# Storing the split projection weights of the prompt block through GpSimd's DMA queue

## The reference, cut to what matters

```
h = _rmsnorm(x, norm_mix_g) * (1.0 + sc1) + sh1
...
proj = jnp.einsum('btd,dc->btc', h, w_in)
```

## Time and profile before

| | |
|---|---|
| runs | 2404.28, 2408.15, 2408.19 us, median 2408.15 |
| span of the profiled execution, first to last instruction | 2406.7 us, 1.45 us under the median; its own time is not listed apart from the runs |
| TensorE / weight load / VectorE / ScalarE / GpSimd busy | 93% / 85% / 69% / 50% / 30% |
| mean granted TensorE clock | 0.969 |
| SP's DMA queue (q1, hardware) | 377.81 MB |
| GpSimd's DMA queue (q0, software) | 126.38 MB |
| prompt block's projection | about 52 to 154 us of the span |

### The profile page before, as it was taken

How to read it: one execution, slowest core, us unless ns; L and a number is a source line. 1 busy time by engine, 2 the same in 40 slices (tenths; PEclk the granted TensorE clock), 3 DMA queues, 4 the chain that set the end, 5 groups by cost and what they waited for, 6 DMA issues and landing times.

```text
span 2406.7 us, 43831 instructions
## 1 busy us (share of the span) xinstructions
PE 2242.9 (93%) x16687; PEld 2055.1 (85%) x16687; DVE 1667.3 (69%) x2936; ACT 1194.0 (50%) x1935; POOL 712.7 (30%) x654
## 2 busy tenths in 40 slices
PE   3889999999996899975999999999999999999995
PEld 3877878788785677763999999999999999999995
DVE  1879979799788766667666655665566656666585
ACT  3766364553524454431545554555445554555574
POOL 1000000000001311101354455544554455534541
PEclk8989999999998999987999999999999999999998
DMA  6987576757747566355476677666775677666986
GB/s 225 370 319 220 200 251 229 263 193 250 236 145 264 158 210 193 106 176 139 149 206 185 193 198 213 188 185 197 197 211 180 179 212 198 199 192 179 299 250 245
DMA packets 291030, 505.80 MB, mean 210 GB/s; under 512 B 27713, under 2 KB 234302, under 8 KB 275296
## 3 DMA queue, kind: packets, MB, share of 16 engines
q1 hardware_dynamic: 251792, 377.81, 48.1%
q0 software_dynamic: 39120, 126.38, 19.4%
HBM read 405.61 MB, written 98.53 MB: 209 GB/s over the span
## 4 chain that ended last, share of the span: by engine, by line
PE 60%; DVE 5%; DMA 2%; issue 1%; ACT 1%; POOL 0%; SPq 0%; DVEq 0%; POOLq 0%; ACTq 0%
PE bank L1650 19%; PE bank L1652 19%; PE bank L1651 19%; DMA out_dram<-work_exp 1%; PE bank L1904 1%; DVE work_exp L2918 1%; DVE work_proj L2558 1%; PE bank L1970 1%; PE bank L1914 1%; PE bank L1922 1%; DVE work_exp L3181 1%; PE bank L1979 0%; POOL cat_hl L1454 0%; DMA work_exp<-x_rows 0%; DVE hl_exp L3097 0%
## 5 line engine op out<-in xcount | busy, mean ns | idle before, releaser
L1650 PE MATMUL bank<-act_hl_exp,hl_exp 128*128 128x288 f32 x3072 | 909.8, 296 | 11.5 <-DVE hl_exp L3097 7.5
L1651 PE MATMUL bank<-act_hl_exp,hl_exp 128*128 128x288 f32 x3072 | 907.5, 295 | 1.0 <-issue 0.8
L1652 PE MATMUL bank<-act_hl_exp,hl_exp 128*128 128x288 f32 x3072 | 905.7, 295 | 0.0
L1650 PEld LDWEIGHTS bank<-act_hl_exp,hl_exp 128*128 128x128 f32 x3072 | 577.2, 188 | 12.5 <-DVE hl_exp L3097 9.0
L1651 PEld LDWEIGHTS bank<-act_hl_exp,hl_exp 128*128 128x128 f32 x3072 | 578.1, 188 | 2.5 <-issue 2.5
L1652 PEld LDWEIGHTS bank<-act_hl_exp,hl_exp 128*128 128x128 f32 x3072 | 579.2, 189 | 0.2 <-issue 0.2
L3097 DVE TENSOR_TENSOR hl_exp<-work_exp,hl_exp 128x1024 fp32r<-128x1024 f32 x192 | 231.3, 1226 | 205.8 <-ACT hl_exp L1238 195.4
L3097 DVE TENSOR_TENSOR hl_exp<-raw_exp,hl_exp 128x1024 fp32r<-128x1024 f32 x192 | 231.4, 1221 | 196.5 <-ACT hl_exp L1238 176.7
L2558 DVE SCALAR_TENSOR_TENSOR work_proj<-work_proj,wcv 128x392 f32<-128x392 f32 (+12 forms) x600 | 338.8, 635 | 1.2
L1238 ACT ACTIVATE hl_exp<-work_exp 128x1024 fp32r<-128x1024 f32 x192 | 199.2, 1054 | 201.3 <-PE bank L1652 199.6
L1238 ACT ACTIVATE hl_exp<-raw_exp 128x1024 fp32r<-128x1024 f32 x192 | 198.6, 1053 | 163.8 <-PE bank L1652 135.4
(11 more groups left out here) (408 smaller groups left out, 3314.3 us busy)
## 6 DMA issues: line engine op xcount, KB each, us to landing
hl_proj<-park_w POOLq DMA_DIRECT2D x80, 1024.0 KB, 6.1
raw_exp<-in_w_e_gate_dram SPq DMA_DIRECT2D x32, 1024.0 KB
raw_exp<-in_w_e_up_dram SPq DMA_DIRECT2D x32, 1024.0 KB
work_exp<-in_w_e_gate_dram SPq DMA_DIRECT2D x32, 1024.0 KB
work_exp<-in_w_e_up_dram SPq DMA_DIRECT2D x32, 1024.0 KB
raw_exp<-in_w_e_down_dram SPq DMA_DIRECT2D x32, 1024.0 KB
work_exp<-in_w_e_down_dram SPq DMA_DIRECT2D x32, 1024.0 KB
park_w<-hl_proj SPq DMA_DIRECT2D x8, 2048.0 KB, 12.2
```

Source lines behind the costliest of these rows:

```text
L1650: pe.matmul(out, lh, rh, start=first, stop=False)
L1651: pe.matmul(out, lh, rl, start=False, stop=False)
L1652: return pe.matmul(out, ll, rh, start=False, stop=last_)
```

## The change

The ten stores leave SP's queue and are issued by GpSimd, in the same order of units and with the same waits for the split. SP keeps its loads and its other stores in the same order. The row loads at the end of the kernel count on another semaphore (`s_st`, used for 32 counts before), because `s_wst2` is now counted by GpSimd's DMAs.

```diff
-        f_x = [Sig(s_wst2, 0, 0, 16 * 8), Sig(sem("f_x1"), 0), Sig(k_T, 0, 0, 2), Sig(k_e, 0, 0, 1)]
+        f_x = [Sig(s_st, 0, 0, 32), Sig(sem("f_x1"), 0), Sig(k_T, 0, 0, 2), Sig(k_e, 0, 0, 1)]
...
                     sp.wait_ge(s_lo[j % 2], 2 * (j // 2) + 2)
                     if j + 2 < NPROJ:
                         load_proj(j + 2)
-                    if SLOT[j] < 2:
-                        sp.dma_start(park_w[j], hl[:, SLOT[j]].bitcast(f32)).then_inc(s_stored[SLOT[j]], 16)
-                        return
-                    for q in range(2):
-                        for i in range(2):
-                            sp.dma_start(park_w[j, :, q, i], w_part(b, j, q, i).bitcast(f32)).then_inc(s_wst2, 16)
...
+            def store_w(b, j):
+                pool.wait_ge(s_lo[j % 2], 2 * (j // 2) + 2)
+                if SLOT[j] < 2:
+                    pool.dma_start(park_w[j], hl[:, SLOT[j]].bitcast(f32)).then_inc(s_stored[SLOT[j]], 16)
+                    return
+                for q in range(2):
+                    for i in range(2):
+                        pool.dma_start(park_w[j, :, q, i], w_part(b, j, q, i).bitcast(f32)).then_inc(s_wst2, 16)
+
             def stage2(b, nb):
 
+                if b.prompt:
+                    for j in range(NPROJ):
+                        store_w(b, j)
```

## The result

The change runs in 2413.18 us (median of 6 runs, 2411.13 to 2416.69), beside 2405.78 us for the kernel before (6 runs, 2404.28 to 2408.19). The ratio is 1.0032 with an interval of 1.0021 to 1.0043: slower by 0.32%. The profiled execution took 2411.13 us, the shortest of the six, with a span of 2409.1 (before: 2406.7, which only the two longest of its six executions, 2408.15 and 2408.19 us, can hold).

The account below looks back on a forecast made before the run. The prediction took the DMA engines to set the pace in the prompt block, 55 to 135 us. Terms of 0 + 0 + 2.4 us made the span 2409.1 and, with 1.45 us more, the median 2410.5 us; range 2404 to 2416.

Parts of the forecast that it names:

- within 0.2%: Whole time against the kernel before: no change a measurement can tell, chance 0.75; slower had 0.20, faster 0.05.
- The size in the prompt block: Unit 9's split at 136.6 us in place of 134.2, +2.4 us; latent block's first matmul near 157.
- store 5 has 256 per engine: Prompt block: SP's loads keep pace with store 5's packets, so store 6 lands up to 4.8 us later.
- The starved loads: Rival, chance 0.15: big store packets delay load 9, or load 6, and so unit 9's split; +4.7 us, 2412.9.
- Slow issue: Rival, chance 0.10: GpSimd needs over 3.5 us per small-piece store instruction, so stores issue late; +5 us and more.
- SP's issue time: Prompt block: SP, freed of stores, issues loads earlier, but the DMA engines are already full; 0 us on the path.
- DMA share: Sign in the prompt block: stays at 1.0 from 55 to 135 us; below 0.95 the prediction is wrong.
- the faster case: Rival, chance 0.10: store 7 lands 1.4 us sooner or two queues use the DMA engines better; 2405.7 us.

Follow-up runs that it names:

- e5: The change, with loads 2 to 9 issued through GpSimd's queue too, in the order of the kernel before: 2406.09 us, ratio 1.0004 to before.
- e9: The kernel before, all on SP's queue, with the store issued ahead of the load for units 0, 1, 3, 4, 6 and 7: 2412.35 us, ratio 1.0027.
- e1: The kernel before with only the semaphore of the late row loads moved, stores staying on SP: 2408.6 us, ratio 1.0004.
- e3: The kernel before with only stores 2 and 5 moved to GpSimd's queue, the big stores staying on SP: 2407.44 us, ratio 1.0004.
- e2: The kernel before with only the eight big stores moved to GpSimd's queue, stores 2 and 5 staying on SP: 2411.24 us, ratio 1.0022.
- e6: The change, with each big store as four DMAs of 4 KB per partition: 2414.01 us, ratio 1.0031 to the kernel before.
- e7: The change, with each big store as sixteen DMAs of 1 KB per partition: 2411.49 us, ratio 1.0022 to the kernel before.
- e4: The change, with GpSimd waiting before each store until the load two units on has landed: 2412.32 us, ratio 1.0025 to the kernel before.

## Why the prediction came out as it did

**The time** was predicted at 2410.5 us in a range of 2404 to 2416, and measured at 2413.18. The likeliest case was "within 0.2%", with 0.75; it became slower by 0.32%, which had 0.20. The change itself was forecast at +2.4 us and is +7.4 us, three times as much. The time came out nearer than that because the forecast started from the median of three runs, 2408.15, and that of six is 2405.78.

**The size in the prompt block was right, and its reason was not.** Split 8 was predicted at 128.9 (measured 128.73), split 9 at 136.6 (136.34), the latent start near 157 (156.60), and +2.4 us stands against +2.12. The step that failed is "store 5 has 256 per engine, ... the loads of SP's queue keep pace packet for packet ... store 6 now lands up to 4.8 us later". Store 5 had 32 packets per engine on GpSimd's queue, and load 8 waited about 4 us for its turn. So the loads lost to the stores: store 6 landed 3.1 us earlier than before, and loads 3 and 8 took 23.1 and 20.1 us (13.4 and 8.5 before). That the same numbers came out is luck: two sums that both end in ScalarE's 7.6 us from split 8 to split 9.

**The starved loads (0.15)** was the mechanism that happened: small packets against big ones, one in turn. Its places were others. I gave it its price at load 9 (+4.7 us), which landed at 132.8 (112.92 + 19.9), before unit 9's split was due, and, as a second place, at load 6, "handed on" by the copy. Unit 6's split is 3.75 us late, but the copy doesn't follow it: it follows TensorE, which starts unit 5 late because it waited for unit 3. The prediction did not see load 3, over 20 us before store 5 is issued, where two big stores already lay beside it. Without the wait of 1.22 us for load 8, unit 8's split would start at 127.51 and unit 9's 7.61 us later, at 135.12: so 0.90 of the +2.12 us come from unit 3, and 1.22 from load 8.

**The order of the data is the cause; this is shown from both sides.** With the loads ahead in one queue, GpSimd's queue costs nothing (e5), and stores ahead of loads on SP's queue, with nothing else changed, cost about as much as the change (e9). e1 takes out the semaphore, and e3 shows that a late load is covered up to a point. Which load becomes late differs from run to run (unit 3 in the change, 5 in e2, 4 in e6 and e7, 2 in e9).

**Slow issue (0.10)** is refuted: 0.89 us for each instruction, where I took 2.4 and set the threshold at 3.5. (The Trainium skill, "SBUF — State Buffer", section Summary: rules for kernel authors, warns that VectorE in its 2x or 4x mode starves GpSimd's descriptor writing. With VectorE busy for 57.33 of the 80 us the slowest of these took 925 ns; the profile doesn't name VectorE's modes, and this trace shows no such stall.)

**SP's issue time** was rightly put at 0 on the path, and SP was "no longer held" at these loads. That load 5 would be issued near 78, load 8 near 104 and park_q behind it was still wrong: they went out at 82.83, 108.54 and 108.96, as units 3 and 6, whose splits they follow, were late themselves.

**DMA share** stayed at 0.97 and above 0.95 as said; the GB/s did not rise, so the faster case had nothing to stand on. (The Trainium skill, "DMA: Bandwidth & Descriptors", section Issuing engines are not separate DMA queues, gives issue time as what a second issuing engine saves, and nothing else. The trace agrees on the saving, load 8 being issued 0.07 us after its split and not 6.5. By that sentence the change would cost nothing; its ratio is 1.0032, as with two issuers the order between their transfers is lost.)

**From +2.1 us in the prompt block to +7.4 us in all.** I had added no term for this to the sum. The kernels fall in two groups: latent start at 154.5 or less with ratios of 1.0000 to 1.0004, and at 156.5 or more with 1.0022 to 1.0032. Three things on record narrow the gap.

First, +2.1 us is low. It stands on one profile of before, whose latent start of 154.48 is the latest of the first group: its six profiles have 152.37 to 154.48 (mean 153.5), the seven of the second group 156.50 to 159.18 (mean 157.6), and the change's two 156.60 and 157.21. Against the mean the change is about 3.4 us late, and the groups are 4.1 us apart.

Second, nothing is lost behind the latent start in the profiled executions: from there to the end of the span it takes 2252.2 us before and 2252.5 after (2406.7 - 154.48, 2409.1 - 156.60), and over the groups 2251.9 and 2251.4 us on average.

Third, the profiled executions are single ones, and over all runs the granted clock differs: 0.9668 on average in the first group (150 runs, mean 2406.8 us) and 0.9655 in the second (66 runs, 2412.3 us). Among the 91 runs of before beside the experiments, those at 0.965 took 2408.8 us (16 runs) and those at 0.967 2406.6 us (35 runs), 1.1 us for each 0.001. By this the clock makes 1.4 us of the 5.5 us between the groups, and the latent start 4.1. This is an estimate from averages, and not a test: within the second group the ratio does not grow with the delay (e9 +2.0 us and 1.0027, e2 +4.1 and 1.0022), and e2 and e7 were slow at a mean clock of 0.966, which e1 and e3 had too. Why the clock is lower in most of the second group stays open. In the profile of the change a lower clock is seen in the prompt block: from 80 to 105 us it is 0.80 where before has 0.86, and from 54 to 157 us TensorE waited 14.1 us (9.8 + 4.3) for split weights, 10.6 us (6.4 + 4.2) before.

No version beat the kernel before; e5 with 1.0004 and the earliest latent start (152.37) comes nearest, and its gain of 2.1 us there (1.1 against the mean of its group) did not show in the whole time.

## What to carry to other kernels

Where the DMA engines are full, one queue's issue order is the priority list. Moving half the transfers to another queue added no bandwidth here (358 GB/s for 368) and gave the order away, and loads in 1 KB packets got 7 to 9% of the time beside stores in 16 KB packets. Before moving a store, look for the loads that stand ahead of it in the old queue and ask what covers each if it comes 5 to 10 us later; here a delay of 4.45 us at one unit was covered (e3) and one of 7.87 us was not (e7). If it must move, move the loads with it (e5), as neither a wait (e4) nor 4 KB packets (e6, e7) brought the time back.

## What the runs showed of the hardware that was not expected

GpSimd's queue joined the 512-byte pieces into packets of 4 KB: 1024 packets for 4 MB where SP's queue sent 8192. The 1 KB pieces of e7's stores and e5's loads went in 4 KB packets too. Its issue of such a DMA took 0.89 us, against 0.56 us for one of 128 pieces. Load 9, issued on SP while load 8 and park_q were still under way, held SP for 10.60 us, longer than any store had (8.73 us in the earlier trace rows). And a load newly issued beside a busy queue got 4 packets in 2 us (110 to 112 us) before its turn came.
